# Seven-product branch projections and output projection, with their combined weights made ahead in DRAM

## The reference, cut to what matters

```python
xn = rmsnorm(x, norm_w)
proj = xn @ w_in                       # (T, 1024) @ (1024, 10248)
q, k, v, i_pre, f_pre, o_pre, z_m, b_g, c_g, x_c, z_c, g_m, g_c = split(proj)
h = mlstm_chunkwise(q, k, v, ig, lf, C0, n0, m0)          # 4 heads
h = h * rsqrt(mean(h * h) + EPS)
h = h.reshape(B, L, 1024) * head_norm_w
h = h * sigmoid(o_pre) * silu(z_m)
y_m = h @ w_proj_m                                        # (T, 1024) @ (1024, 1024)
cv = short_conv(c_g * x_c, conv0, conv_w)
y_c = (silu(z_c) * b_g * cv) @ w_proj_c                   # (T, 1024) @ (1024, 1024)
mix = sigmoid(g_m) * y_m + sigmoid(g_c) * y_c
out = x + mix @ w_out                                     # (T, 1024) @ (1024, 1024)
y = rmsnorm(out, final_norm_w)
```

## Time and profile before

| what | value |
|---|---|
| median of three runs | 2359.93 us (2356.53, 2359.93, 2360.93) |
| span of the profiled execution | 2356.7 us |
| granted TensorE clock, mean | 0.998 of full (2.4 GHz) |
| PE busy / DVE busy / ACT busy | 99% / 63% / 40% |
| phase A / B / C / D with tail | 216 / 1566.5 / 373.9 / 200.3 us |
| DMA | 425.66 MB, mean 181 GB/s |

### The profile page before, as it was taken

One profiled execution on the slowest core, in us unless ns is written; L12 is line 12 of the kernel. 1 busy time (PEld: TensorE's weight loads), 2 busy tenths in 40 slices (PEclk: granted clock), 3 DMA queues, 4 the chain that ended last, 5 costly groups with the idle time before them and its releaser, 6 DMA issues. The chain is left out here.

```text
span 2356.7 us, 41040 instructions
## 1 busy us (share of the span) xinstructions
PE 2323.1 (99%) x14643; PEld 2254.8 (96%) x14643; DVE 1488.1 (63%) x2703; ACT 948.6 (40%) x1717; POOL 77.5 (3%) x84
## 2 busy tenths in 40 slices
PE   8999999999999999999999999999999999999998
PEld 8998999999999999999999999999998999998886
DVE  4447788898876687777776677777755333324333
ACT  3224444444454444455655444555554101002121
POOL 0011000000110000000020000000000000000000
PEclk9999999999999999999999999999999999999999
DMA  6665655455775765656765766557567433443442
GB/s 224 209 215 136 199 187 181 157 177 176 232 220 174 232 202 184 191 159 195 240 191 177 235 202 195 188 175 217 176 185 260 156 102 110 138 143 126 138 138 86
DMA packets 424977, 425.66 MB, mean 181 GB/s; under 512 B 32810, under 2 KB 363690, under 8 KB 424870
## 3 DMA queue, kind: packets, MB, share of 16 engines
q1 hardware_dynamic: 424870, 424.25, 56.9%
HBM read 297.36 MB, written 126.85 MB: 180 GB/s over the span
## 5 line engine op out<-in xcount | busy, mean ns | idle before, releaser
L1658 PE MATMUL b_g<-x_hi,w_hi 128*128 128x344 f32 (+1 forms) x3024 | 985.5, 326 | 9.0 <-DVE rows L1333 4.3
L1658 PE MATMUL b_g<-x_lo,w_hi 128*128 128x344 f32 (+1 forms) x3024 | 967.9, 320 | 0.0
L1658 PE MATMUL b_g<-x_hi,w_lo 128*128 128x344 f32 (+1 forms) x3024 | 967.0, 320 | 0.0
L1658 PEld LDWEIGHTS b_g<-x_hi,w_hi 128*128 128x128 f32 x3024 | 569.3, 188 | 16.1 <-DVE rows L1333 4.4
L1658 PEld LDWEIGHTS b_g<-x_lo,w_hi 128*128 128x128 f32 x3024 | 569.3, 188 | 1.7
L1658 PEld LDWEIGHTS b_g<-x_hi,w_lo 128*128 128x128 f32 x3024 | 569.4, 188 | 0.0
L1155 ACT ACTIVATE w_hi<-w_operands 128x512 fp32r<-128x512 f32 x519 | 323.5, 628 | 272.9 <-PE b_g L1658 261.2
L1295 DVE TENSOR_TENSOR w_lo<-w_operands,w_hi 128x512 fp32r<-128x512 f32 x519 | 354.2, 695 | 1.2
L1155 ACT ACTIVATE w_hi<-stages 128x512 fp32r<-128x512 f32 x216 | 134.7, 629 | 138.3 <-PE b_g L1658 119.4
L1295 DVE TENSOR_TENSOR w_lo<-stages,w_hi 128x512 fp32r<-128x512 f32 x216 | 145.6, 684 | 7.7 <-ACT w_hi L1155 6.9
L2017 PE MATMUL c_g<-act_hi,RH 128*128 128x294 f32 x448 | 134.4, 300 | 2.1 <-DVE rows L1948 2.1
(11 more groups left out here) (305 smaller groups left out, 3116.0 us busy)
## 6 DMA issues: line engine op xcount, KB each, us to landing
w_operands<-w_in SPq DMA_DIRECT2D x282, 256.0 KB, 5.2
stages<-w_ops_d SPq DMA_DIRECT2D x36, 768.0 KB, 5.5
w_operands<-w_ops_d SPq DMA_DIRECT2D x34, 768.0 KB, 4.9
stages<-w_in SPq DMA_DIRECT2D x72, 256.0 KB, 3.8
w_operands<-w_ops_d SPq DMA_DIRECT2D x70, 256.0 KB, 6.3
w_ops_d<-w_operands SPq DMA_DIRECT2D x18, 768.0 KB, 3.3
w_ops_d<-stages SPq DMA_DIRECT2D x18, 768.0 KB, 3.4
w_ops_d<-w_operands SPq DMA_DIRECT2D x36, 256.0 KB, 3.9
```

Source lines behind the costliest of these rows:

```text
L1658: last = nc.tensor.matmul(bank[:, 0:n], w[:, j, k, :], x[:, k, 0:n], start=(j < 4 and k == 0 and m == 0), stop=(k == 3 and m == 2), skip_g ...
```

## The change

Phases C and D become one stage, `phase_cd`, and both use the seven-product form. For a branch, two blocks of 128 output columns (b and b + 4) times two groups of 258 tokens make a unit of seven products with 4 x 3 matmuls; two units are interleaved, product by product, each with its four PSUM banks (`for u in range(NU)`, NU = 16). That makes 32 x 7 x 12 = 2688 matmuls of 258 columns. The output product takes two tiles of 128 tokens and two halves of 512 columns at once: 8 x 7 x 12 = 672 matmuls, and 48 for the sample tokens.

The seven combined operands of the 12 weight blocks (4 of each of `w_proj_m`, `w_proj_c`, `w_out`) are made in the first pass of phase B. For block b SP loads four quarters of 256 KB into `kT`, `qT`, `neg_max` and `h` and copies three quarters from DRAM to DRAM (`load_weights`, L1025, L1027), DVE makes four sums of 128x512 (`projection_sum`, L1521 on, at products 5 to 8 of the body's 14), and SP stores four results (`store_sums`) to `proj_d`. This is done in one body each of oz 1 to 3, conv 0 to 7 and gates 0. Later `load_operand` brings an operand straight to where its low part will stand, and the split writes in place. The activation quarters are combined by DVE (`act_sum`, three to four sums per group of 258 x 2 tokens), and split as before.

`head_norm_w` is no longer multiplied into the weights, but by an additional ACT copy into the oz rows (24 times). The first branch's gated rows are stored to `mix_d`; the second branch's are added to it in DRAM by POOL's DMAs with an adding store (`accumulate`). Each row buffer holds 528 KB. The DMAs for the first operands of the new stage are issued at the end of phase B, while its last pairs still run, and the first splits stand in the last pair. The eight warm-up matmuls at L2023 and the block boundary between C and D are gone.

```diff
--- before.py
+++ after.py
...
-TN = 294
-NTC = 7
-TP = TN * NTC
+TN = 258
+NG = 4
+TP = 2 * TN * NG
+NU = 4 * NG
+NT2 = L // (2 * P)
+NW = 12
+BANK = (0, 1, 2, 3, 0, 2, 3)
+SPLIT_AT = {1: 4, 2: 45, 3: 56, 4: 101, 5: 108}
...
-        phase_c(nc, g)
-        phase_d(nc, g)
+        phase_cd(nc, g)
...
+def weight_block(g, b):
+
+    return (g.w_proj_m, g.w_proj_c, g.w_out)[b // 4], b % 4 * P, D // 2 + b % 4 * P
...
+def load_acts(eng, g, s):
+    if s < 2 * NG:
+        src, n, c0 = (g.hg_d, g.cv_d)[s // NG], TN, s % NG * 2 * TN
+    else:
+        src, n, c0 = g.mix_d, P, (s - 2 * NG) * 2 * P
+    for slot, k0, c in ((0, 0, c0), (1, 0, c0 + n), (2, 4, c0 + n), (4, 4, c0)):
+        eng.dma_start(act_block(g, s, slot), src[k0:k0 + 4, :, c:c + n].rearrange("k p n -> p k n")).then_inc(act_signal(g, s)[0], 16)
+
+
+def act_sum(nc, dve, g, s, at):
...
+def act_sum(nc, dve, g, s, at):
+
+    a, b, c, d, e = (act_block(g, s, slot) for slot in range(5))
+    if at == 0:
+        dve.wait_ge(*act_signal(g, s))
+        nc.vector.tensor_tensor(b, c, b, ALU.subtract).then_inc(g.xq_sum, 1)
+    elif at == 1:
+        dve.wait_ge(g.xq_sum, 4 * s + 1)
+        nc.vector.tensor_tensor(d, b, a, ALU.add).then_inc(g.xq_sum, 1)
+    elif at == 2:
+        dve.wait_ge(g.x_ready, 7 * s + 1)
+        dve.wait_ge(g.xq_sum, 4 * s + 2)
+        nc.vector.tensor_tensor(a, c, d, ALU.subtract).then_inc(g.xq_sum, 1)
+    else:
+        dve.wait_ge(g.x_ready, 7 * s + 2)
+        dve.wait_ge(g.xq_sum, 4 * s + 3)
+        nc.vector.tensor_tensor(d, e, d, ALU.subtract).then_inc(g.xq_sum, 1)
+
+
+def act_source(g, s, j):
...
+            def load_weights(b):
+
+                if b:
+                    sp.wait_ge(q_out, 16 * NOP * b)
+                w, c0, c1 = weight_block(g, b)
+                w = w[0].rearrange("(k p) n -> p k n", p=P)
+                for place, k0, c in zip(raw_pieces, (0, 0, 4, 4), (c0, c1, c0, c1)):
+                    sp.dma_start(place, w[:, k0:k0 + 4, c:c + P]).then_inc(q_in, 16)
+                for j, k0, c in ((0, 0, c0), (4, 4, c0), (5, 4, c1)):
+                    sp.dma_start(g.proj_d[b, :, j], w[:, k0:k0 + 4, c:c + P]).then_inc(q_out, 16)
+
+            def store_sums(b):
+                sp.wait_ge(q_set, 4 * (b + 1))
+                for place, j in zip(raw_pieces[1:], (2, 6, 1, 3)):
+                    sp.dma_start(g.proj_d[b, :, j], place).then_inc(q_out, 16)
+
...
+                if s == "gates" and i == 0 and p == 2:
+                    sp.wait_ge(r_ready, 7 * 3)
+                    sp.wait_ge(q_out, 16 * NOP * NW)
+                    load_acts(sp, g, 0)
+                if block_of(p, s, i) is not None:
+                    load_weights(block_of(p, s, i))
...
-                        nc.scalar.activation(ZT[:, 0:n], ER[:, q, 1, 0:n], ACT.Tanh, scale=0.5).then_inc(z_set, 1)
+                        nc.scalar.activation(ZT[:, 0:n], ER[:, q, 1, 0:n], ACT.Tanh, scale=0.5)
+                        nc.scalar.activation(ER[:, q, 1, 0:n], ER[:, q, 1, 0:n], ACT.Copy,
+                                             scale=g.hnw[:, bass.ds(2 * i + q, 1)]).then_inc(z_set, 1)
...
+            def projection_sum(b, at):
+
+                r0, r1, r2, r3, t = raw_pieces
+                if at == 0:
+                    dve.wait_ge(q_in, 64 * (b + 1))
+                    nc.vector.tensor_tensor(t, r1, r3, ALU.add).then_inc(q_set, 1)
+                elif at == 1:
+                    dve.wait_ge(q_set, 4 * b + 1)
+                    nc.vector.tensor_tensor(r3, t, r0, ALU.subtract).then_inc(q_set, 1)
+                elif at == 2:
+                    nc.vector.tensor_tensor(r1, r0, r1, ALU.subtract).then_inc(q_set, 1)
+                else:
+                    dve.wait_ge(q_set, 4 * b + 2)
+                    nc.vector.tensor_tensor(r2, r2, r3, ALU.subtract).then_inc(q_set, 1)
...
+                        if block_of(p, s, i) is not None and 5 <= 7 * q + j < 9:
+                            projection_sum(block_of(p, s, i), 7 * q + j - 5)
...
+            def accumulate(n):
+                pool.wait_ge(gated, n + 1)
+                pool.dma_start(two_rows(g.mix_d, n), MX[n % 2], accum_op=ALU.add).then_inc(g.acc_out[n % 2], 16)
...
+            def branch_product(n, j):
+                br, t, p = place(n)
+                if t == 0:
+                    pe.wait_ge(g.w_ready, split_count(4 * br + p, j))
+                if p == 0:
+                    pe.wait_ge(g.x_ready, 7 * (n // 4) + j + 1)
+                if n > 1:
+                    bank_free(n - 2, j, copies, parts_made)
+                bank_read(n, j, copies, parts_made)
+                high, low = act_parts(g, n // 4, j)
+                bank = G[4 * (n % 2) + BANK[j]]
+                for k in range(4):
+                    for m, (w, x) in enumerate(((0, high), (0, low), (1, high))):
+                        last = nc.tensor.matmul(bank[:, 0:TN], g.W[:, p, j, w, k, :], x[:, k, :],
+                                                start=(j < 4 and k == 0 and m == 0), stop=(k == 3 and m == 2),
+                                                skip_group_check=True)
                 last.then_inc(done, 1)
 
-            tile(0, 0)
...
+            for u in range(NU):
+                for j in range(NOP):
+                    branch_product(2 * u, j)
+                    branch_product(2 * u + 1, j)
```

More of the change, by code:

```diff
@@ new lines, in phase_cd @@
+    N = D // 2
+    at = g.places
+    tail = g.XS[:, :, :, :].rearrange("p s k n -> p (s k n)")[:, 20 * TN:26 * TN].rearrange("p (a n) -> p a n", n=TN)
+    TG = [at_place(nc, "tanh_gate", [P, 2, 2 * TN], at["gate"])[:, :, :], tail[:, 0:4].rearrange("p (a h) n -> p a (h n)", a=2)]
+    P1 = [tail[:, 4], tail[:, 5]]
+    parts = at_place(nc, "c_part", [P, 2, TN], at["part"])
+    U2 = [parts[:, 0], parts[:, 1]]
+    rows = g.ER[:, :, :, :].rearrange("p q r n -> p q (r n)")
+    MX = [rows[:, q, 0:4 * TN].rearrange("p (a n) -> p a n", a=2) for q in range(2)]
@@ new lines, in y_stored, with two_rows, row_free, behind @@
+    def y_stored(i):
+        return 16 * (NU // 2 + i // 2 + 1)
+    def two_rows(a, n):
+        _, t, p = place(n)
+        return a.rearrange("(a b) p n -> b p a n", a=2)[p][:, :, t * 2 * TN:(t + 1) * 2 * TN]
+    def row_free(eng, n):
+        if n < 2:
+            eng.wait_ge(g.row_out[n], g.rows_stored[n])
+        elif n - 2 < NU:
+            eng.wait_ge(rows_out[n % 2], 16 * ((n - 2) // 2 + 1))
+        else:
+            eng.wait_ge(g.acc_out[n % 2], 16 * ((n - 2 - NU) // 2 + 1))
+    def behind(u, j):
+        found = split_behind(u, j)
+        return [(2 * found[0] + q, found[1]) for q in range(2)] if found else []
@@ new lines, in _ @@
+            for u in range(NU):
+                for j in range(NOP):
+                    step(2 * u, j)
+                    step(2 * u + 1, j)
+                    if u == 0 and 1 <= j < 4:
+                        split_high(nc, act, g, 0, j + 3)
+                        act_high(nc, act, g, 0, j + 3)
+                        split_high(nc, act, g, 1, j + 3)
+                    for b, o in behind(u, j):
+                        split_high(nc, act, g, b, o)
+                    if u % 2:
+                        act_high(nc, act, g, u // 2 + 1, j)
@@ L2012, in _ @@
+            last.then_inc(summed, 1)
+            variance(NT2)
+            normed(NT2, 0)
         @block.tensor
         def _(pe):
[L2014 to L2020 removed]
@@ new lines, in _ @@
+            pe.wait_ge(sx_set, 3)
+            pe.wait_ge(copied, out_copies(NT2 - 2, 4))
+            pe.wait_ge(ev, out_parts(NT2 - 2, 1))
+            for h, operands in enumerate((((0, 0), (1, 4)), ((0, 3), (2, 5)))):
+                count = 0
+                for a, j in operands:
+                    for k in range(4):
+                        for x, w in ((SH, 0), (SH, 1), (SL, 0)):
+                            last = nc.tensor.matmul(G[h][:NS, :], x[:, a, k, :], g.W[:, :, j, w, k, :],
+                                                    start=(count == 0), stop=(count == 23))
+                            count += 1
@@ L2219, in phase_d @@
+            last.then_inc(d_done, 1)
     ctx.close()
```

869 lines of the change are left out of this document (480 added, 389 removed).

## The result

| | before | after |
|---|---|---|
| median | 2360.28 us | 2435.32 us (2433.15 to 2440.02, 4 runs) |
| ratio | 1 | 1.0326 (95%: 1.0312 to 1.0341) |
| profiled span | 2356.7 us | 2430.2 us |
| granted clock, mean | 0.998 | 0.978 |

A forecast was written before the change was run, and what follows sets the result against it. PE's matmul pace was taken as the bound, with DVE bounding first-pass bodies once it waits. Span 2356.7 - 42.5 - 22.3 + 0 + 67.5 = 2359.4 us, median 3.2 above, rounded 2363; range 2325 to 2395.

The forecast's parts named there:

- the first loss: First pass of phase B: DVE's added sums and its wait for their quarters in twelve bodies, +67.5 us.
- So it waits 5.8 us: First pass, oz and conv bodies: DVE's wait for the four raw quarters before its first projection sum.
- 14.4 was forecast: Gates 0, first pass: DVE waits 5.8 + 8.6 = 14.4 us, as SP issues the quarters of x first.
- about 0.35: Conv bodies: added loads, copies and stores as a share of a body, giving DMA share 0.87, no saturation on average.
- the extra ACT copy in the oz rows: Oz rows: 0.7 us on an engine at 40%, before a DVE row multiplication with slack, cost 0.
- The step that failed: Second branch: a row buffer is wanted again after 20 us, 10 of them free for the adding store, cost 0.
- about 3.0: Adding stores: us for a plain store of 528 KB; about 6 if reading the old values costs as much again.
- the rival with 0.15: Second branch: adding stores landing after more than 10 us hold up buffer copies and PE, +24, so 2387; chance 0.15.
- 0.119 us at 258 columns: Branch stage: matmuls of 258 columns were forecast to follow at 0.120 us.
- -22.3: Output stage: 816 matmuls become 720, 96 x 0.2324 = -22.3 us.
- the stretch up to the output: End of phase B to the first output matmul: -42.5 us, from 2688 narrower branch matmuls.
- the first stretch: Up to the end of phase B: forecast term +67.5 us.

The follow-up runs named there:

- experiments 1 and 4: 1: the changed kernel with loads at the body's head (2363.8 us) or sums at products 9 to 12 (2370.8); 4: 24 matmuls added in conv 3 to 7 (2436.4).
- Experiment 3: The changed kernel with each block's three DRAM to DRAM copies issued at the end of the body instead of right behind its loads: 2443.3 us.
- experiment 5: The changed kernel with second-branch stores by POOL without addition (2404.3 us), by SP without it (2402.4), or adding with four row buffers (2403.8).

## Why the prediction was wrong

- **The place and the mechanism of the first loss were right.** DVE's wait for quarters that SP issues behind a store, the evacuation behind it in DVE's order, DVE's chain as the bound: experiments 1 and 4. **Its size was not**: "So it waits 5.8 us" measured 5.8 to 5.9 in oz, but 6.3 in conv 0 and 7.1 to 7.6 in the other conv bodies, and gates 0 had 15.2 where 14.4 was forecast. Over all twelve that is 12.7 us. I had priced the four loads by bytes in a stretch without copies and left the copies, issued right behind, out of their landing time, though I had counted them in the mean share. (That share has a slip: 3.84 of loads, as much again for the copies and 2.6 for the stores are 0.39 of a body of 26.6, not "about 0.35". The windows give 10 us, 0.70 x 34.0 less 0.52 x 26.5, and no saturation on average.) Experiment 3 gives the copies 1.0 us of the wait; the rest is open. Another 0.8 us of each conv body are small gaps that a sum of busy time and wait leaves out. The last 6 us lie in the two later passes, where the extra ACT copy in the oz rows had been put at 0.
- **The step that failed** is "A row buffer is wanted again one unit later, 2 x 84 x 0.120 = 20 us, of which 10 are free for the store: 0." A unit has two adding stores, and I treated them as running at once, as the plain stores of the first branch do. They run one behind the other, so the second landed 14 to 20 us after the first was issued (17 after its rows were gated, in the unit shown). Cost: 31 to 33 us (experiment 5); PE's waits alone are 30.3, or 3.8 a unit. Two sizes in this step were off as well: one adding store takes 8.8 us, not 6, and a plain one of the first branch 8.6, not "about 3.0", and the room was about 8 us, not 10. They cost little: plain stores that land in 7.4 to 8.0 us leave PE 2.4 us of waiting in the second branch. It was the rival with 0.15, which named the right place and the right waiting copy and was priced at +24. But its condition, that each store lands after more than 10 us, is not what happened.
- **What was right:** 0.119 us at 258 columns; -21.2 for the output stage against -22.3. Of the 44.8 us by which the stretch up to the output missed, 12 to 14 are not the adding stores'. Seen there are 4.6 and 0.9 us of idle time at the start, a half clock behind them, and some 4 us in the first branch for row buffers; they were not taken apart further.
- **The range** held the two costs as alternatives, forecast or second rival, never both. That alone would not have broken it: their sum, 2363 + 24 = 2387, lay inside. The sizes broke it: the first stretch came out 25 us over its term and the second 45.

The Trainium skill ("SBUF — State Buffer", section "SBUF: two separate sides") had led me to look at a port that DVE shares and can hold against the writing of descriptors for POOL's DMAs. No run shows that here: DVE's gating instruction takes 1.23 us in the first branch, without POOL's DMAs, and 1.23 to 1.24 in the second, and without the addition POOL issues its DMAs 1.3 us apart. The wait was for the stores' landing.

The Trainium skill ("DMA: Bandwidth & Descriptors", section "Anatomy of one DMA — SWDGE (gpsimd) path") gives 2.0 us + bytes/436e3 for a DMA from POOL. That would be 3.2 us for 528 KB, an estimate. The traces have 7.4 without the addition and 8.8 with it, beside other traffic, and they decide.

## What to carry to other kernels

Where an engine that works in order and is nearly full gets a new wait, the whole chain behind it pays in every round. Try first to move the transfer's issue ahead of SP's own waits: it took one edit and brought back 71.5 us here. Then look where the moved transfer now stands in the way (7.4 us in the next gates body). Give buffers that a slow store releases a spare. Ask of each new kind of transfer not only how long one takes but whether two run at once. And if two priced risks are independent, put their sum in the range, with each at more than its middle size.

## What the runs showed of the hardware

- In seven of the eight pairs of adding stores of 528 KB issued by POOL the second is issued 9.5 to 10.4 us behind the first, each time some 0.3 us after that has landed; plain ones from the same queue follow at 1.3 or less.
- One plain store of 528 KB lands in 8.6 us when SP issues it and in 7.4 when POOL does, an adding one in 8.8 (medians, beside other traffic).
- PE's clock fell to 1.2 GHz in a pause of 4 us and stayed there for 5 us of work; matmuls of 344 columns then follow at 0.287 us instead of 0.158. Where another engine's chain was the bound, filling the pause brought the clock back and no time.
- A load of four 256 KB blocks behind 1.34 MB of stores, with 0.75 MB of DRAM to DRAM copies behind it, had landed 7.8 us after its first issue.
